# The last feed-forward group of each layer, reordered by chunk: up 0, up 1, down 0, up 2, down 1, down 2

## The chip, the core and the metric

One Trainium2 chip, one of its cores. The metric is the device time of one execution in microseconds. The engines: TensorE (PE in the profile, PEld for its weight loads), VectorE (DVE), ScalarE (ACT), GpSimd (POOL) and SyncE (SP), which issues most of the transfers.

## What is computed

One inference step of a hybrid streaming encoder with two layers, for 1024 frames of a new stream and 64 of a running one. Each layer is a mixer (attention) and a squared-ReLU MLP, each between two RMSNorms:

```
def rmsnorm(x, g):
    y = xf * lax.rsqrt(jnp.mean(xf * xf, axis=-1, keepdims=True) + NORM_EPS)
    return (y * g.astype(jnp.float32)).astype(x.dtype)

def squared_relu_mlp(h, w_up, w_down):
    u = jax.nn.relu(h @ w_up)
    return (u * u) @ w_down

xp = xp + rmsnorm(mp, g_post_mix[l])
xp = xp + rmsnorm(squared_relu_mlp(rmsnorm(xp, g_pre_ffn[l]), w_ffn_up[l], w_ffn_down[l]), g_post_ffn[l])
```

D_MODEL is 1024, D_FF 4096; after the MLP of layer 0 the norm `g_pre_mix` of layer 1 follows at once.

## The kernel before, in words

Everything is feature-major: 1088 tokens lie along the free axis, in three chunks of 384, 384 and 320 columns (`CHUNKS`). A product in float32 is made of three passes over split operands: high times high, low times high, high times low. So a weight unit of 128x1024 is loaded into a stage `WS` (three stages, `STAGE = [0, 1, 2, 0]`, so units 0 and 3 share one), cast to its high part `WH` by ScalarE (`hi_unit`, L685) and split into its low part `WL` by GpSimd (`lo_unit`, L541). There are four slots of `WH` and `WL`; a set of four units is called a quad. A load waits until the split of the unit that had its stage is over; a cast waits until TensorE has finished its last use of the slot (semaphore `D`).

The MLP runs in eight groups per layer, each over 512 of the 4096 hidden features. A group is 24 steps of 24 matmuls (L1273): 12 up steps (3 chunks of 4 units), each giving one result in PSUM, then 12 down steps, each giving two results; six PSUM banks are used in turn. VectorE empties an up result into `TU`, squares it, and makes the low part of `U` (L1200, L1203, L1206); it adds a down result to `ACC` (L1220). Before the change each quad serves all three chunks: the splits for the down quad are made during the up steps of chunk 2, those of the next group during the down steps of chunk 2.

The last group of a layer carries the norm behind the MLP as well. ScalarE squares each finished row of `ACC` into `SQ` (L715), GpSimd sums the squares (`sum_square`, L576 and L579, eight per chunk). Then for each chunk, in this order and on these engines: `post_load` (GpSimd issues the load of the residual XRES), `post_stat` (TensorE, statistics matmul, L1253), `post_st` (VectorE, L934), `post_pow` (GpSimd, power, L556), `post_dg` (VectorE, diagonal, L944), `post_bc` (TensorE, broadcast matmul, L1260), two halves of `post_x0`, `post_x1` (VectorE scales 4 rows and adds them to the residual, L953 and L958), `post_store`. In layer 0 the norm ahead of the next layer follows for each chunk: `pre_hi`, `pre_sq` (ScalarE), `pre_lo` and the reductions `pre_red0`, `pre_red1` down to `PSX` (VectorE, L963, L922, L926, L930), `pre_stat`, `pre_st`, `pre_pow`, `pre_dg`, `pre_bc`, `pre_rb`. Then the projections of layer 1 (section T0) begin.

Where each piece stands on its engine is fixed by a table: `PLAN` gives a tick for each piece, `LATER` an offset by chunk, and each engine calls `norm_at` or (TensorE) `norm_until` between its own steps, one step per tick; tick 0 of chunk 0 is the first down step of chunk 1. Each engine works strictly in its written order, and semaphores release it.

## Time and profile before

| | us |
|---|---|
| median of 3 runs | 3023.59 |
| lowest and highest | 3022.15, 3024.40 |
| the profiled execution | 3024.18 |
| its span | 3022.4 |

The page gives, over the span, TensorE busy 2836.2 us (94%), VectorE 1446.0 (48%), ScalarE 854.1 (28%), GpSimd 686.5 (23%), and 210.32 MB moved at a mean of 70 GB/s. Line L1273 (all dense matmuls) makes up 69% of the chain that ended last. Times in the rows below are counted from the span's start: layer 0's last feed-forward group begins at 1434.53, layer 1's at 2892.03.

### The profile page before, as it was taken

To read this page: it belongs to the slowest core of one execution; us is meant where nothing else is said; L and a number is where in the kernel's file an instruction comes from. 1 tells how busy PE (TensorE), PEld (TensorE's weight loads), DVE (VectorE), ACT (ScalarE), POOL (GpSimd) and SP (SyncE) were. 2 spreads that over 40 slices of the span, in tenths; PEclk is the share of its full clock that TensorE was granted. 3 is DMA by queue.
4 is the path that set the end of the run, shared out by engine and by line. 5 is a ranking of instruction groups with operands and counts; after the bars stand their busy time and mean duration, and the time that the engine had idled before them with its cause. 6 is when DMAs were issued, how large, how long until landed. Compare 5 with 4: busy or idle time off the path is not lost.

```text
span 3022.4 us, 49537 instructions
## 1 busy us (share of the span) xinstructions
PE 2836.2 (94%) x18736; PEld 2711.3 (90%) x18736; DVE 1446.0 (48%) x3541; ACT 854.1 (28%) x1561; POOL 686.5 (23%) x436
## 2 busy tenths in 40 slices
PE   5799999998999999999979999998889999999996
PEld 5788888888999999999978888887889999999996
DVE  4466655555633333333385566555573333333334
ACT  3344433354211111111233333335431111111121
POOL 1111210155211212122231110005432212122123
PEclk8899999999999999999989999999999999999998
DMA  4211211233201111010231121113411111010103
GB/s 149 99 56 55 73 70 74 87 111 141 82 35 49 35 49 56 28 56 35 72 119 60 66 96 57 57 57 121 157 67 56 36 49 55 28 56 35 49 36 119
DMA packets 58381, 210.32 MB, mean 70 GB/s; under 512 B 6888, under 2 KB 16496, under 8 KB 54816
## 3 DMA queue, kind: packets, MB, share of 16 engines
q1 hardware_dynamic: 54400, 168.95, 15.8%
q0 software_dynamic: 3888, 40.11, 3.3%
q8 instruction: 61, 1.00, 0.1%
q14 instruction: 32, 0.26, 0.0%
HBM read 163.36 MB, written 51.97 MB: 71 GB/s over the span
## 4 chain that ended last, share of the span: by engine, by line
PE 82%; DVE 6%; issue 4%; ACT 2%; POOL 1%; DMA 0%; DVEq 0%; ACTq 0%; POOLq 0%
PE ps L1273 69%; PE ps L1369 3%; PE ps L1387 3%; PE ps L1334 2%; DVE XL L963 1%; PE ps L1383 1%; PE ps L1344 1%; PE ps L1346 1%; DVE ACC L953 1%; PE ps L1354 1%; ACT Kh L853 1%; DVE PR L1073 1%; PE ps L1260 1%; ACT Qh L849 1%; POOL XL L630 0%
## 5 line engine op out<-in xcount | busy, mean ns | idle before, releaser
L1273 PE MATMUL ps<-XH,WH 128*128 128x384 f32 (+1 forms) x3096 | 1032.2, 333 | 51.6 <-DVE XL L963 22.3
L1273 PE MATMUL ps<-XL,WH 128*128 128x384 f32 (+1 forms) x3096 | 1035.1, 334 | 0.0
L1273 PE MATMUL ps<-XH,WL 128*128 128x384 f32 (+1 forms) x3096 | 1028.6, 332 | 0.0
L541 POOL TENSOR_TENSOR WL<-WS,WH 128x1024 fp32r<-128x1024 f32 x209 | 508.2, 2436 | 1805.3 <-ACT WH L685 1710.4
L1273 PE MATMUL ps<-U,WH 128*128 128x384 f32 (+1 forms) x3072 | 757.5, 330 | 0.0
L1273 PEld LDWEIGHTS ps<-XH,WH 128*128 128x128 f32 x3096 | 589.5, 190 | 60.4 <-issue 46.3
L1273 PEld LDWEIGHTS ps<-XL,WH 128*128 128x128 f32 x3096 | 589.6, 190 | 11.8 <-issue 11.8
L1273 PEld LDWEIGHTS ps<-XH,WL 128*128 128x128 f32 x3096 | 589.5, 190 | 9.4 <-issue 9.4
L1273 PEld LDWEIGHTS ps<-U,WH 128*128 128x128 f32 x3072 | 547.1, 189 | 0.0
L1273 PE MATMUL ps<-U,WL 128*128 128x384 f32 (+1 forms) x1536 | 506.7, 330 | 0.0
L685 ACT CAST WH<-WS 128x1024 fp32r<-128x1024 f32 x209 | 217.9, 1045 | 651.9 <-PE ps L1273 628.2
L1220 DVE TENSOR_TENSOR ACC<-ps,ACC 128x384 f32<-128x384 f32 (+1 forms) x336 | 178.2, 535 | 429.9 <-PE ps L1273 429.9
L772 ACT ACTIVATE PR<-PR,NM 128x640 f32<-128x640 f32 (+8 forms) x288 | 206.6, 717 | 376.3 <-DVE NM L1078 367.4
L1200 DVE SCALAR_TENSOR_TENSOR TU<-ps,RB 128x384 f32<-128x384 f32 (+1 forms) x192 | 102.7, 535 | 406.8 <-PE ps L1273 406.8
L1273 PEld LDWEIGHTS ps<-U,WL 128*128 128x128 f32 x1536 | 290.0, 189 | 0.0
L893 ACT ACTIVATE U<-TU 128x384 fp32r<-128x384 f32 (+1 forms) x192 | 97.6, 508 | 617.3 <-DVE TU L1200 617.3
L1073 DVE CUSTOM_DVE_ANT_0 PR<-ps,BIAS 128x640 f32<-128x640 f32 (+8 forms) x288 | 196.1, 681 | 80.5 <-issue 76.3
L1083 DVE COPY PT<-ps 128x640 f32<-128x640 f32 (+7 forms) x120 | 73.7, 623 | 200.1 <-PE ps L1369 199.8
L1369 PE MATMUL ps<-ident,PR 128*128 128x128 f32 (+1 forms) x996 | 134.2, 275 | 1.3 <-DVE M L1073 1.3
L778 ACT COPY PT<-ps 128x640 f32<-128x640 f32 (+8 forms) x160 | 85.1, 542 | 153.0 <-PE ps L1369 152.8
L1369 PEld LDWEIGHTS ps<-ident,PR 128*128 128x128 f32 (+1 forms) x996 | 116.2, 141 | 7.8 <-DVE M L1073 2.6
L1387 PE MATMUL ps<-PT,V 128*64 128x128 f32 (+1 forms) x1680 | 117.3, 280 | 2.3 <-ACT PT L778 2.3
(119 smaller groups left out, 2141.5 us busy)
## 6 DMA issues: line engine op xcount, KB each, us to landing
WS<-w_in SPq DMA_DIRECT2D x209, 512.0 KB, 4.5
k_out<-KT SPq DMA_DIRECT2D x16, 672.0 KB, 3.3
x_scr<-XRES POOLq DMA_DIRECT2D x6, 1536.0 KB, 5.5
XRES<-x_scr POOLq DMA_DIRECT2D x6, 1536.0 KB, 7.1
v_out<-VT SPq DMA_DIRECT2D x16, 544.0 KB, 4.8
o_scr<-OT SPq DMA_DIRECT2D x14, 544.0 KB, 2.7
XRES<-x_in POOLq DMA_DIRECT2D x4, 1536.0 KB, 9.4
BIAS<-nc_scr SPq DMA_DIRECT2D x8, 672.0 KB, 4.8
```

The costliest lines, as they stand in the source:

```text
L541: pool.tensor_tensor(WL[u][:, :], WS[STAGE[u]][:, :], WH[u][:, :].bitcast(f32), ALU.subtract)\
L685: act.copy(WH[u][:, :], WS[st][:, :]).then_inc(sem["whi"], 1)
L772: act.activation(PR[:, s % 2, m, 0:n], PR[:, s % 2, m, 0:n], ACT.Exp, bias=NM[:, q:q + 1], accum_out=L[:, q:q + 1]).then_inc(sem["ex"], 1)
L778: ins = act.copy(dst, src)
L893: act.activation(ct(U, c, u), TU[:, t % 2, 0:w], ACT.Square).then_inc(sem["uhi"], 1)
L1073: dve.tensor_tensor_reduce(out=PR[:, s % 2, m, 0:n].rearrange("p (b w) -> p b w", b=nb), in0=ps[:, 2 + 2 * m:2 + 2 * m + nb, 0:n // nb], i ...
L1083: ins = dve.tensor_copy(dst, src)
L1200: dve.scalar_tensor_tensor(out=TU[:, t % 2, 0:w], in0=ps[:, t % 6, 0:w], scalar=0.0, in1=RB[:, o:o + w], op0=ALU.max, op1=ALU.mult).then_i ...
L1220: dve.tensor_tensor(acc, ps[:, v % 6, 0:w], acc, ALU.add).then_inc(sem["evD"], 1)
L1273: return pe.matmul(bank[:, 0:w], wt, xt, start=m == 0, stop=m == 3 * tiles - 1, skip_group_check=False)
L1369: ins = pe.transpose(both(m)[0:v, n * P:(n + 1) * P], PR[:, k % 2, m, o:o + v], ident[:, :])
L1387: ins = pe.matmul(ps[f, 6, 0:P], V[0:v, t, f], PT[0:v, m, o // P, :], **ends)
```

## The change

The order of the 24 steps in the last group of each layer becomes up 0, up 1, down 0, up 2, down 1, down 2 by chunk. Since there are only four slots, the up quad is loaded and split again for up 2, and the down quad again for down 1 and 2. The norm pieces of chunk 0 behind the MLP and ahead of layer 1 stand four ticks earlier (`LATER`), so that they begin in up 2, and chunk 0's pre-norm stands ahead of chunk 1's post-norm in the order of jobs. The other groups keep their order. The weight list on the host gets the last eight units of each layer twice.

```diff
+def ff_steps(last):
+
+    order = (("up", 0), ("up", 1), ("dn", 0), ("up", 2), ("dn", 1), ("dn", 2)) if last else [(w, c) for w in ("up", "dn") for c in range(3)]
+    out, j = [], 0
+    for what, c in order:
+        for u in range(4):
+            out.append((what, c, u, j))
+            j += 1 if what == "up" else 2
+    return out
+
+
+def ff_quads(last):
+
+    return [1, 2, 3, 5] if last else [2, 5]
+
+
+def ff_result(last, what, c, u=0):
+    return next(j for w, k, v, j in ff_steps(last) if (w, k, v) == (what, c, u))
...
-            per = add(dict(D=36, evD=36, uhi=12, um=12, uu=12, whi=4 + nxt, wlo=4 + nxt), quad, stage_loads(range(nxt)))
-            out.append(Section("FF", layer, reps, per, units=8, f=f, last=last, nxt=nxt))
+            more = len(ff_quads(last)) - 1
+            per = add(dict(D=36, evD=36, uhi=12, um=12, uu=12, whi=4 * more + nxt, wlo=4 * more + nxt), *([quad] * more), stage_loads(range(nxt)))
+            out.append(Section("FF", layer, reps, per, units=4 + 4 * more, f=f, last=last, nxt=nxt))
...
-        for c, part in (((0, "post"), (0, "pre"), (1, "post"), (2, "post"), (1, "pre"), (2, "pre")) if n % 2 else
-                        ((0, "post"), (1, "post"), (0, "pre"), (2, "post"), (1, "pre"), (2, "pre"))) if part in NORMS[n]]
+        for c, part in ((0, "post"), (0, "pre"), (1, "post"), (2, "post"), (1, "pre"), (2, "pre")) if part in NORMS[n]]
...
-LATER = [(0, 4, 8), (-10.5, 0, 4)]
+LATER = [(-4, 4, 8), (-10.5, 0, 4)]
...
-                        load_quad(sec, i, 0)
-                        load_quad(sec, i, 4, sec.nxt)
+                        for q in range(len(ff_quads(sec.last))):
+                            load_quad(sec, i, 4 * q, 4 if q < len(ff_quads(sec.last)) - 1 else sec.nxt)
...
-                    pool.wait_ge(sem["D"], section("FF", n // 2 - 1, True).at(None, "D", 12 + 8 * (c + 1)))
+                    pool.wait_ge(sem["D"], section("FF", n // 2 - 1, True).at(None, "D", ff_result(True, "dn", c) + 8))
...
-                        for t in range(12):
-                            if t >= 8:
-                                lo_unit(sec, i, t - 8, t - 8)
-                            if sec.f == 0:
-                                norm_at(1 + 2 * sec.layer, NORM_ON_FF + t)
-                        for t in range(12):
-                            if sec.last:
-                                sum_square(2 + 2 * sec.layer, 2 * t)
-                                sum_square(2 + 2 * sec.layer, 2 * t + 1)
-                                norm_at(2 + 2 * sec.layer, t - 3)
-                            if t >= 8 and t - 8 < sec.nxt:
-                                lo_unit(sec, i, 4 + t - 8, t - 8)
+                        for p, (what, c, u, j) in enumerate(ff_steps(sec.last)):
+                            if what == "dn" and sec.last:
+                                for v in (8 * c + 2 * u, 8 * c + 2 * u + 1):
+                                    sum_square(2 + 2 * sec.layer, v)
+                            if p // 4 in ff_quads(sec.last):
+                                q = ff_quads(sec.last).index(p // 4)
+                                if 4 * q + u < sec.per["wlo"]:
+                                    lo_unit(sec, i, 4 * q + u, u)
+                            if sec.f == 0 and what == "up":
+                                norm_at(1 + 2 * sec.layer, NORM_ON_FF + p)
+                            if sec.last and p >= 11:
+                                norm_at(2 + 2 * sec.layer, p - 15)
...
+                            for k in range(2) if what == "dn" and sec.last else ():
+                                act.wait_ge(sem["evD"], sec.at(i, "evD", j + k + 1))
+                                square(2 + 2 * sec.layer, 2 * t + k, ct(ACC, c, 2 * u + k)).then_inc(sem["sqo"], 1)
+                            if p // 4 in ff_quads(sec.last):
+                                q = ff_quads(sec.last).index(p // 4)
+                                if 4 * q + u < sec.per["wlo"]:
+                                    uses = (2 if STAGE[u] == 0 else 1) * q + (2 if u == 3 else 1)
+                                    hi_unit(sec, i, 4 * q + u, u, uses, sec.at(i, "D", j + (1 if what == "up" else 2)))
+                            if sec.f == 0 and what == "up":
+                                norm_at(1 + 2 * sec.layer, NORM_ON_FF + p)
+                            if sec.last and p >= 11:
+                                norm_at(2 + 2 * sec.layer, p - 15)
...
+                        firsts = [0] + [4 * (q + 1) for q in ff_quads(sec.last)[:-1]]
+                        for p, (what, c, u, j) in enumerate(ff_steps(sec.last)):
+                            if p // 4 * 4 in firsts:
+                                weights(sec, i, 4 * firsts.index(p // 4 * 4) + u)
+                            if what == "up":
+                                if j < 6 and sec.f == 0:
+                                    pe.wait_ge(sem["evA"], sec.at(i, "evA", j - 5))
+                                else:
+                                    pe.wait_ge(sem["evD"], sec.at(i, "evD", j - 5))
+                                if sec.f == 0 and u == 0:
+                                    h_ready(1 + 2 * sec.layer, c)
+                                if sec.f == 0:
+                                    step(ps[:, j % 6, :], c, u, 1 + 2 * sec.layer, NORM_ON_FF + p)
+                                elif sec.last and p >= 11:
+                                    step(ps[:, j % 6, :], c, u, 2 + 2 * sec.layer, p - 15)
+                                else:
+                                    step(ps[:, j % 6, :], c, u)
+                                continue
                             if u == 0:
                                 pe.wait_ge(sem["uu"], sec.at(i, "uu", 4 * (c + 1)))
-                            for v in (2 * t, 2 * t + 1):
-                                pe.wait_ge(sem["evD"], sec.at(i, "evD", 7 + v))
+                            for k in range(2):
+                                pe.wait_ge(sem["evD"], sec.at(i, "evD", j + k - 5))
                                 for m in range(N_MM // 2):
                                     if sec.last and m % 6 == 0:
-                                        norm_until(2 + 2 * sec.layer, t - 4 + (v % 2) / 2 + m / N_MM)
-                                    ins = product(ps[:, v % 6, :], CHUNKS[c][1], c, u, 4 * (v % 2), m, U, 4, (U, 4))
+                                        norm_until(2 + 2 * sec.layer, p - 16 + k / 2 + m / N_MM)
+                                    ins = product(ps[:, (j + k) % 6, :], CHUNKS[c][1], c, u, 4 * k, m, U, 4, (U, 4))
...
+            if f == FF_GROUPS - 1:
+                out += out[-8:]
```

VectorE's loop is rewritten in the same manner over `ff_steps`.

GpSimd, from down 0's first sum of squares in layer 0's last group (RB is where the sums are kept, RS the power's result). Before:

```order
L576 COPY RB<-SQ 128x384
L579 TENSOR_TENSOR RB<-RB,SQ 128x384 x7
L551 DMA XRES<-x_scr 128x3072
L576 COPY RB<-SQ 128x384
L579 TENSOR_TENSOR RB<-RB,SQ 128x384
L556 TENSOR_TENSOR RS<-ST,halfpow 128x3
```

The same engine from the same place now (its lines are numbered 20 higher):

```order
L596 COPY RB<-SQ 128x384
L599 TENSOR_TENSOR RB<-RB,SQ 128x384
L561 TENSOR_TENSOR WL_55<-WS_59,WH_51 128x1024
L599 TENSOR_TENSOR RB<-RB,SQ 128x384 x2
L561 TENSOR_TENSOR WL_56<-WS_60,WH_52 128x1024
L599 TENSOR_TENSOR RB<-RB,SQ 128x384 x2
L561 TENSOR_TENSOR WL_57<-WS_61,WH_53 128x1024
L599 TENSOR_TENSOR RB<-RB,SQ 128x384 x2
L561 TENSOR_TENSOR WL_58<-WS_59,WH_54 128x1024
L571 DMA XRES<-x_scr 128x3072
L561 TENSOR_TENSOR WL_55<-WS_59,WH_51 128x1024
L576 TENSOR_TENSOR RS<-ST,halfpow 128x3
```

A split stands behind each pair of sums, and a fifth split, the first for down 1, stands between the load of the residual and chunk 0's power; before, two sums of chunk 1 stood there.

VectorE, from down 0's eight results in layer 0's last group. Before:

```order
L1220 TENSOR_TENSOR ACC<-ps,ACC 128x384 x8
L934 TENSOR_SCALAR ST<-ps 128x3
L1220 TENSOR_TENSOR ACC<-ps,ACC 128x384 x2
L944 TENSOR_SCALAR DG<-ident,RS 128x128 x3
L953 SCALAR_TENSOR_TENSOR ACC<-ACC,G,ps 128x384 x4
L958 TENSOR_TENSOR XRES<-XRES,ACC 128x1536
L1220 TENSOR_TENSOR ACC<-ps,ACC 128x384 x2
```

The same engine and place now:

```order
L1234 TENSOR_TENSOR ACC<-ps,ACC 128x384 x8
L951 TENSOR_SCALAR ST<-ps 128x3
L1216 SCALAR_TENSOR_TENSOR TU<-ps,RB 128x320
L1219 TENSOR_TENSOR TS<-TU 128x320
L1222 TENSOR_TENSOR U<-TS,U 128x320
L961 TENSOR_SCALAR DG<-ident,RS 128x128 x3
L970 SCALAR_TENSOR_TENSOR ACC<-ACC,G,ps 128x384 x4
L975 TENSOR_TENSOR XRES<-XRES,ACC 128x1536
```

Between the norm pieces stand the three passes over a result of up 2, where the two adds of a down step of chunk 1 stood.

GpSimd at chunk 1's power, from the first sum of chunk 2's squares, layer 0. Before:

```order
L576 COPY RB<-SQ 128x320
L579 TENSOR_TENSOR RB<-RB,SQ 128x320
L556 TENSOR_TENSOR RS<-ST,halfpow 128x3
L541 TENSOR_TENSOR WL_55<-WS_59,WH_51 128x1024
L579 TENSOR_TENSOR RB<-RB,SQ 128x320 x2
```

The same engine and place now:

```order
L596 COPY RB<-SQ 128x320
L599 TENSOR_TENSOR RB<-RB,SQ 128x320
L561 TENSOR_TENSOR WL_55<-WS_59,WH_51 128x1024
L576 TENSOR_TENSOR RS<-ST,halfpow 128x3
L599 TENSOR_TENSOR RB<-RB,SQ 128x320 x2
```

The first split of the next layer's weights has moved ahead of the power; in layer 1 there is no such split.

## Rows read from the trace of the kernel before

**Rows 1.** The page, part 1: busy time, share of the span, instructions.
```profile
PE 2836.2 (94%) x18736; PEld 2711.3 (90%) x18736; DVE 1446.0 (48%) x3541; ACT 854.1 (28%) x1561; POOL 686.5 (23%) x436
```

**Rows 2.** Busy time per window, end of layer 0's last group: PE, PEld, DVE, ACT, POOL.
```profile
1509.00:1524.00 15.00, 13.40 (x82) 13.14 (x80) 14.19 (x20) 7.41 (x13) 4.98 (x5) 1.00 0.08 32
...
1524.00:1540.00 16.00, 9.69 (x50) 9.46 (x51) 11.42 (x18) 4.16 (x6) 6.98 (x7) 0.68 0.53 200
...
1540.00:1553.00 13.00, 10.09 (x67) 9.77 (x66) 12.93 (x17) 9.06 (x15) 9.82 (x8) 1.00 0.22 83
```

**Rows 3.** What TensorE waited for, 1430 to 1620: total, times, longest.
```profile
PE ps L1253 <- issue: 6.3, 1, 6.3
...
PE ps L1253 <- POOL RB L579: 6.3, 1, 6.3
...
PE ps L1260 <- DVE DG L944: 5.8, 3, 2.9
```

**Rows 4.** Timeline of TensorE, both layers: start, us, what, idle before.
```profile
1434.53 0.34 PE L1273 MATMUL ps<-XH,WH 128*128 128x384 f32 x1
...
1528.75 1.41 PE L1253 MATMUL ps<-ones,RB 128*128 128x1 f32 x6 [6.34 <-issue]
...
1536.51 0.94 PE L1260 MATMUL ps<-DG,ones 128*128 128x128 f32 x6 [1.56 <-DVE DG L944]
...
1560.38 1.29 PE L1253 MATMUL ps<-ones,RB 128*128 128x1 f32 x6 [6.28 <-POOL RB L579]
...
2892.03 0.34 PE L1273 MATMUL ps<-XH,WH 128*128 128x384 f32 x1
...
2988.09 1.09 PE L1260 MATMUL ps<-DG,ones 128*128 128x128 f32 x6
...
3003.24 1.31 PE L1253 MATMUL ps<-ones,RB 128*128 128x1 f32 x6 [6.14 <-POOL RB L579]
```

**Rows 5.** Timeline of GpSimd, layer 0.
```profile
1473.57 2.40 POOL L541 TENSOR_TENSOR WL<-WS,WH 128x1024 fp32r<-128x1024 f32 x1 [35.32 <-ACT WH L685]
...
1477.09 2.40 POOL L541 TENSOR_TENSOR WL<-WS,WH 128x1024 fp32r<-128x1024 f32 x1 [1.12 <-ACT WH L685]
...
1487.55 1.00 POOL L579 TENSOR_TENSOR RB<-RB,SQ 128x384 f32<-128x384 f32 x1 [0.58 <-ACT SQ L715]
...
1489.67 1.01 POOL L579 TENSOR_TENSOR RB<-RB,SQ 128x384 f32<-128x384 f32 x1 [1.11 <-ACT SQ L715]
...
1532.76 0.88 POOL L556 TENSOR_TENSOR RS<-ST,halfpow 128x3 f32<-128x3 f32 x1
```

**Rows 6.** Timeline of VectorE, layer 0.
```profile
1471.56 0.49 DVE L1200 SCALAR_TENSOR_TENSOR TU<-ps,RB 128x320 f32<-128x320 f32 x1 [1.74 <-PE ps L1273]
...
1507.68 0.68 DVE L944 TENSOR_SCALAR DG<-ident,RS 128x128 f32<-128x128 f32 x3 [2.70 <-POOL RS L556]
...
1514.22 2.18 DVE L953 SCALAR_TENSOR_TENSOR ACC<-ACC,G,ps 128x384 f32<-128x384 f32 x4
...
1533.67 2.79 DVE L944 TENSOR_SCALAR DG<-ident,RS 128x128 f32<-128x128 f32 x3 [2.51 <-POOL RS L556]
...
1540.12 1.76 DVE L958 TENSOR_TENSOR XRES<-XRES,ACC 128x1536 f32<-128x1536 f32 x1
...
1547.35 2.61 DVE L944 TENSOR_SCALAR DG<-ident,RS 128x128 f32<-128x128 f32 x3
...
1549.88 7.40 DVE L963 SCALAR_TENSOR_TENSOR XL<-XRES,G,XH 128x384 fp32r<-128x384 f32 x8
```

**Rows 7.** Timeline of ScalarE, layer 0: a cast.
```profile
1472.46 1.04 ACT L685 CAST WH<-WS 128x1024 fp32r<-128x1024 f32 x1
```

**Rows 8.** Weight loads in 1200 to 1500, issue to landing.
```profile
DMA to landing us min/median/max: 3.3/4.2/5.7
```

**Rows 9.** Windows of 2 us; the number after POOL's is TensorE's granted clock.
```profile
1528.00:1530.00 2.00, 1.25 (x6) 1.28 (x7) 1.70 (x1) 0.27 (x1) 1.16 (x2) 0.50 0.27 49
...
1534.00:1536.00 2.00, 0.95 (x5) 0.69 (x3) 2.00 (x2) 0.00 (x0) 1.98 (x1) 0.86 0.02 6
```

More of the change, by code:

```diff
@@ L1210, in _ @@
[L1210 to L1222 removed]
+                        for p, (what, c, u, j) in enumerate(ff_steps(sec.last)):
+                            t, (o, w) = 4 * c + u, CHUNKS[c]
+                            if what == "up":
+                                dve.wait_ge(sem["D"], sec.at(i, "D", j + 1))
+                                if sec.f == 0:
+                                    scaled(1 + 2 * sec.layer, c)
+                                if t >= 2 or sec.base.get("uhi", 0):
+                                    dve.wait_ge(sem["uhi"], sec.at(i, "uhi", t - 1))
+                                dve.scalar_tensor_tensor(out=TU[:, t % 2, 0:w], in0=ps[:, j % 6, 0:w], scalar=0.0, in1=RB[:, o:o + w],
+                                                         op0=ALU.max, op1=ALU.mult).then_inc(sem["evD"], 1)
+                                dve.wait_ge(sem["evD"], sec.at(i, "evD", j + 1))
+                                dve.tensor_tensor(TS[:, t % 2, 0:w], TU[:, t % 2, 0:w], TU[:, t % 2, 0:w], ALU.mult).then_inc(sem["um"], 1)
+                                dve.wait_ge(sem["um"], sec.at(i, "um", t + 1))
+                                dve.wait_ge(sem["uhi"], sec.at(i, "uhi", t + 1))
+                                dve.tensor_tensor(ct(U, c, 4 + u), TS[:, t % 2, 0:w], ct(U, c, u).bitcast(f32), ALU.subtract)\
+                                    .then_inc(sem["uu"], 1)
+                                if sec.f == 0:
+                                    norm_at(1 + 2 * sec.layer, NORM_ON_FF + p)
+                            for k in range(2) if what == "dn" else ():
+                                dve.wait_ge(sem["D"], sec.at(i, "D", j + k + 1))
+                                acc, bank = ct(ACC, c, 2 * u + k), ps[:, (j + k) % 6, 0:w]
+                                if sec.f == 0:
+                                    dve.tensor_copy(acc, bank).then_inc(sem["evD"], 1)
+                                else:
+                                    dve.wait_ge(sem["evD"], sec.at(i, "evD", ff_result(False, "dn", c, u) + k + 1 - 36))
+                                    dve.tensor_tensor(acc, bank, acc, ALU.add).then_inc(sem["evD"], 1)
+                            if sec.last and p >= 11:
+                                norm_at(2 + 2 * sec.layer, p - 15)
@@ L1283, in weights @@
             def weights(sec, i, u):
-                per = {"ATT": 3, "FF": 8}.get(sec.kind, 0)
+                per = {"ATT": 3, "FF": sec.units}.get(sec.kind, 0)
                 pe.wait_ge(sem["wlo"], sec.pick(i, sec.unit + u + 1, per))
@@ L1456, in _ @@
                     with runs(pe, sec) as i:
-                        for t in range(12):
-                            c, u = t // 4, t % 4
-                            if t < 6 and sec.f == 0:
-                                pe.wait_ge(sem["evA"], sec.at(i, "evA", t - 5))
-                            else:
-                                pe.wait_ge(sem["evD"], sec.at(i, "evD", t - 5))
-                            if c == 0:
-                                weights(sec, i, u)
-                            if sec.f == 0 and u == 0:
-                                h_ready(1 + 2 * sec.layer, c)
-                            if sec.f == 0:
-                                step(ps[:, t % 6, :], c, u, 1 + 2 * sec.layer, NORM_ON_FF + t)
-                            else:
-                                step(ps[:, t % 6, :], c, u)
@@ L1471, in _ @@
-                        for t in range(12):
-                            c, u = t // 4, t % 4
-                            if c == 0:
-                                weights(sec, i, 4 + u)
+                        firsts = [0] + [4 * (q + 1) for q in ff_quads(sec.last)[:-1]]
+                        for p, (what, c, u, j) in enumerate(ff_steps(sec.last)):
+                            if p // 4 * 4 in firsts:
+                                weights(sec, i, 4 * firsts.index(p // 4 * 4) + u)
+                            if what == "up":
+                                if j < 6 and sec.f == 0:
[4 more added lines that the diff above has]
+                                    h_ready(1 + 2 * sec.layer, c)
+                                if sec.f == 0:
+                                    step(ps[:, j % 6, :], c, u, 1 + 2 * sec.layer, NORM_ON_FF + p)
[4 more added lines that the diff above has]
+                                continue
```

55 lines of the change are left out of this document (4 added, 51 removed).

## The prediction

> **What bounds the kernel now.** I read the page first: TensorE is busy 2836.2 us, 94% of the span [rows 1]. A change that moves no matmul out of the program can only move TensorE's idle time, so I looked for where it idles around the last feed-forward group of each layer. The windows over the end of layer 0's group show it [rows 2]: from 1509 on TensorE is busy 13.40 of 15, 9.69 of 16 and 10.09 of 13 us, while VectorE is busy 14.19, 11.42 and 12.93. The waits of TensorE there [rows 3] are all of the norm: 6.3 and 6.3 us at the statistics matmul (L1253), 5.8 us in three pieces at the broadcast (L1260). The reader should see that VectorE is nearly full there and that TensorE waits, in order, for small norm pieces at fixed places of its program.
>
> TensorE's own rows give two clocks of the stretch [rows 4]. Call the group's first matmul 0 (1434.53 in layer 0, 2892.03 in layer 1). The last statistics matmul (chunk 2) comes at 1560.38 = 125.8 in layer 0 and 3003.24 = 111.2 in layer 1. What lies behind these two has the same order before and after, so the change is worth what these two numbers move by.
>
> Step lengths: a step (24 matmuls) of chunk 2 takes 3.52 us (the splits on GpSimd follow each other at 1473.57 and 1477.09) and a result of a 384 wide down step 2.12 us, so a down step 4.24 (sums at 1487.55 and 1489.67) [rows 5]. The ninth up result is emptied at 1471.56 [rows 6], 37.03 after 0: less one step of 3.52 and 0.1 for the release, the eight before took 4.16 each. Without any wait the group takes 4.16 x 8 + 3.52 x 4 + 4.24 x 8 + 3.52 x 4 = 95.4 us, in either order.
>
> **The change, part by part.** No matmul is added. Added per layer are eight weight units: eight loads, eight casts (1.04 us on ScalarE) and eight splits on GpSimd (2.40 us) [rows 5, 7]. In the old order one set of splits has a whole group of steps to hide in; now down 0 and up 2 each have to cover one, and down 0 also has the eight sums of squares.
>
> A split is finished how late? Result emptied at 1471.56, so done by TensorE at 1471.45; split over at 1475.97: 4.5 us after the last use [rows 5, 6]. So the four splits for down 0, made during up 1 (16.6 to 33.3), end at 25.3, 29.5, 33.6 and 37.8. The next load into the shared stage 0 is issued at 37.8. Landing takes 3.3 to 5.7 us, median 4.2 [rows 8]; I take 4.7, since three go out together: 42.5. Cast 43.6, first split over at 46.1. From here GpSimd works without a pause, by its new order: three times two sums (2.12 us, taken from their spacing; 1.0 busy each) and one split, 46.1 + 3 x (2.15 + 2.4) = 59.7. The splits are over at 46.1, 50.7, 55.2 and 59.7; up 2's steps begin at 50.2, 53.8, 57.3 and 60.8, so the weights themselves come in time by 4 down to 1 us.
>
> The norm does not. **(a) Statistics of chunk 0** now stand at the start of up 2's second step, 53.8, and need the eighth sum, 57.3: TensorE idles 3.6 us. After an idle of 6.3 [rows 3] the rows show TensorE at half clock from 1528.75 to about 1534.6 (granted 0.50, then 0.86 in the window 1534 to 1536), 5.8 us in which half is lost [rows 9]; I count 2.7 us for each idle over about 2 us.
>
> **(b) Broadcast of chunk 0.** It stands three quarters into the same step: 18 matmuls of 0.147 at half clock, after a statistics matmul of 1.41, from 57.4: reached at 64.0. It needs the diagonal of VectorE, and that needs the power on GpSimd, and GpSimd's row ahead of the power is now the first split for down 1. That split needs a load that can be issued only when the fourth split above frees stage 0, at 59.7. So: issue 59.8, landed 65 (5.2, in the upper half of [rows 8], the residual's 1536 KB go out at the same time), cast 66.1, split 68.5, power 0.88 [rows 5], diagonal 0.68 [rows 6]: 70.1. Idle 6.1 us. Step 2 then ends, partly at half clock, at 73.8, step 3 at 78.6, up 2 at 82.1 where 64.3 was the count without waits.
>
> **(c) VectorE behind (b), layer 0 only.** It stands in line at the same diagonal. Then by its new order: half of the scaling 2.2, the residual add 1.8, up result 2 (three passes of 0.49 and two releases between them, some 1.9), again 4.0, up result 3, the low part of chunk 0's input (some 6 with the wait for ScalarE; it took 7.40 [rows 6]), up result 4, the first reduction (an add of the same size as the residual's, and 1.5 of waiting for ScalarE), two down results, the other two reductions: 72.0 + 4.0 + 1.9 + 4.0 + 1.9 + 6.0 + 1.9 + 3.3 + 0.9 + 1.8 = 97.7. The pre-statistics of chunk 0 stand a quarter into down 1's third step, 82.1 + 2 x 4.24 + 1.1 = 91.7. Idle 6.0, and half clock behind it: 1.4 for the statistics, 5.7 for the step's other 18 matmuls, 4.24 for the fourth step; down 1 ends at 109.0.
>
> **(d) Chunk 1.** Its statistics stand after the first step of down 2, at 113.5 with chunk 0's pre-broadcast in it, and nothing is late for them. The broadcast follows 2.6 later. Before, from the end of the statistics to the broadcast took 1530.16 to 1536.51, 6.35, of which the diagonal took 2.79 where it otherwise takes 0.68 [rows 4, 6]; without that 4.2. In layer 0 GpSimd now also has a split before the power (2.4): 6.6, so idle 4.0, and it ends at 122.6 (1.84 at half clock is my allowance). From the end of the broadcast to the last statistics took 1560.38 - 1537.45 = 22.9 before, with a diagonal of 2.61 at 1547.35 [rows 6] that is now gone: 20.4. Last statistics at about 143.0 against 125.8: **layer 0 +17.2 us**.
>
> **(e) Layer 1** has (a) and (b) but no (c): down 2's first step ends at 82.1 + 4 x 4.24 + 3.52 = 102.6; statistics 0.7, the chain 4.2, broadcast 0.9: 108.4. From there to the last statistics it took 14.1 before (2988.09 + 1.09 to 3003.24) [rows 4], with the same work on every engine. That is 122.5 against 111.2: **layer 1 +11.3 us**.
>
> **Moved for nothing.** The loads (16 of 512 KB) add 8 MB over the run on queues that stand idle there, and the order of the other groups stays. The tail behind the last statistics is the same row by row.
>
> Sum: 17.2 + 11.3 = 28.5 on the profiled execution's 3024.18, so 3052.7; the median run is 0.6 lower, so **3052 us**.
>
> A rule that could make it worse: the Trainium skill, "SBUF — State Buffer", section "Who interferes with whom", says that a VectorE instruction with two SBUF inputs, or in a two-port mode, and a GpSimd instruction that reads SBUF shut each other out, whoever starts first holding the port pair for its whole length. The trace agrees where they meet: the diagonal at 1533.67 took 2.79 us beside a split and 0.68 at 1507.68 without one [rows 6]. By that rule alone four meetings of a norm piece with a new split would cost up to 2.4 each, and the sum would be 3062 instead of 3053.
>
> **The rivals.**
> 1. *Forecast*: as summed. Bounds: loads at 3.3 instead of 4.7 and 5.2 us shorten (a) by 1.4 and (b) by 1.9, and if (a)'s idle leaves the clock up another 2.7 goes, in each layer, so -12; (c) may be 3 shorter. Upwards: splits met by VectorE at 2.1 us each (2.79 - 0.68), three times in layer 0 and once in layer 1, +8.4; first load of (b) held up 3 us more by the residual's transfer, +6. That is 3037 to 3067. Chance 0.68.
> 2. *Layer 0 gets its own back*: in the old order VectorE was the limit from 1509 to 1553 [rows 2]; with chunk 0's 18 us of norm gone earlier, the 6.3 at the last statistics disappears and (d) has no wait: 17.2 - 6.3 - 2.7 - 4.0 = +4, with layer 1 +11: 3039 at (e) in full, 3031 with (a) and (b) short. Against it: VectorE has everything of chunk 0 behind (b), so it is not early. Chance 0.12, 3028 to 3037.
> 3. *Faster*: the power isn't held by the split. It decides whether (b) is over by 60.6, when TensorE would reach it at full clock; then layer 0 loses the 6.3 at the statistics of chunk 1, the longest of its three broadcast waits, 2.9 [rows 3], and one half clock, 11.9, and layer 1 about 5: 3007. Against it: the split stands ahead of the power in GpSimd's order and its load cannot start before 59.7. Chance 0.04.
> 4. *The waits feed each other*: half clock delays the result that frees the weights, which delays the split, which delays the power; three such rounds of 5 to 8 us in layer 0 and two in layer 1 on top: 3070 to 3095. Chance 0.12.
> 5. *Nothing measurable*: the extra waits and the relief cancel, 3024. Chance 0.04.
>
> A measurement of this kernel can tell about 0.2%, 6 us. Below 3018 lie rival 3 and a share of 5: 0.05; within, 0.03; slower 0.92. The range that holds 8 in 10 reaches from rival 2's upper part over the forecast to the lower part of rival 4: 3034 to 3072.
>
> **What would show it.** (a) Statistics matmul about 57 us after each group's first matmul, 3 to 4 us idle. (b) Broadcast at about 70, idle about 6, with the split and its load ahead of the power on GpSimd. (c) In layer 0 a wait of about 6 at the first matmul that reads PSX. (d) 4 us at chunk 1's broadcast, 6 again at the last statistics. Last statistics at 143 and 122.5. Four or five stretches at granted clock 0.50 in layer 0 where there were two. The prediction is wrong if the first split for down 1 comes before 62, if up 2 has to wait for weights at every step, or if VectorE has caught up by down 2.

## The result and the profile after

| | us |
|---|---|
| before, median of 4 runs beside it | 3023.99 (3022.15 to 3025.09) |
| changed, median of 4 runs | 3049.85 (3048.40 to 3051.39) |
| ratio, 95% interval | 1.0086 (1.0069 to 1.0104) |
| profiled execution, span | 3048.4, 3046.6 |

Slower by 0.86%, 26 us; the forecast was 3052. The span grew by 24.2 us. The page after, part 1, as in [rows 1]:

```profile
PE 2840.6 (93%) x18736; PEld 2715.6 (89%) x18736; DVE 1451.7 (48%) x3541; ACT 869.5 (29%) x1577; POOL 724.7 (24%) x452
```

The matmuls are the same 18736. ScalarE and GpSimd have the 16 casts and splits more, 15 and 38 us of work; TensorE's busy time grew by 4.4 us only, so the rest of the 24.2 is idle. The same windows as in [rows 2]:

```profile
1509.00:1524.00 15.00, 13.43 (x81) 13.11 (x79) 13.36 (x19) 9.39 (x15) 6.33 (x4) 1.00 0.25 106
1524.00:1540.00 16.00, 10.35 (x49) 10.35 (x50) 8.46 (x14) 3.90 (x8) 9.22 (x9) 0.79 0.30 107
1540.00:1553.00 13.00, 9.18 (x62) 8.92 (x61) 2.20 (x7) 2.82 (x5) 6.29 (x7) 0.94 0.45 163
```

VectorE's load has gone down (12.93 to 2.20 us in the last), and TensorE is no busier for it. What TensorE waited for from 1430 to 1620, as in [rows 3]:

```profile
PE ps L1267 <- POOL RB L599: 11.9, 2, 9.4
PE ps L1274 <- DVE DG L961: 11.0, 2, 7.2
PE ps L1267 <- DVE PSX L947: 7.2, 1, 7.2
```

Statistics and broadcast again, and a new one, chunk 0's pre-statistics (which read PSX): 30.1 us against 18.4. Where they stand, in TensorE's timeline, as in [rows 4] (L1287 are the dense matmuls, L1267 statistics, L1274 broadcast):

```profile
1434.39 0.34 PE L1287 MATMUL ps<-XH,WH 128*128 128x384 f32 x1
...
1490.83 0.80 PE L1267 MATMUL ps<-ones,RB 128*128 128x1 f32 x6 [2.49 <-POOL RB L599]
...
1501.57 1.65 PE L1274 MATMUL ps<-DG,ones 128*128 128x128 f32 x6 [7.20 <-DVE DG L961]
...
1529.65 1.44 PE L1267 MATMUL ps<-ones,PSX 128*128 128x1 f32 x6 [7.22 <-DVE PSX L947]
...
1544.15 0.72 PE L1267 MATMUL ps<-ones,RB 128*128 128x1 f32 x6
...
1551.45 1.65 PE L1274 MATMUL ps<-DG,ones 128*128 128x128 f32 x6 [3.82 <-DVE DG L961]
...
1575.46 1.28 PE L1267 MATMUL ps<-ones,RB 128*128 128x1 f32 x6 [9.43 <-POOL RB L599]
...
2908.98 0.34 PE L1287 MATMUL ps<-XH,WH 128*128 128x384 f32 x1
...
2965.51 0.80 PE L1267 MATMUL ps<-ones,RB 128*128 128x1 f32 x6 [2.58 <-POOL RB L599]
...
2976.13 1.65 PE L1274 MATMUL ps<-DG,ones 128*128 128x128 f32 x6 [7.09 <-DVE DG L961]
...
3027.78 1.31 PE L1267 MATMUL ps<-ones,RB 128*128 128x1 f32 x6 [6.14 <-POOL RB L599]
```

From the group's first matmul to the last statistics: layer 0 141.07 (125.85 before, +15.2), layer 1 118.80 (111.21, +7.6). From layer 0's last statistics to the first matmul of layer 1's last group 1333.52 against 1331.65, +1.9, and from layer 1's last statistics to the end 18.8 against 19.2. With a start 0.1 earlier that is the 24.2 of the span.

GpSimd after, layer 0 (L561 split, L571 residual's load, L576 power); the splits made during down 0, which are the up set for up 2, alternate with pairs of sums. Shown are the first and the fourth of them, the residual's load, the first split for down 1 (the fifth) and the power:

```profile
1477.08 2.41 POOL L561 TENSOR_TENSOR WL<-WS,WH 128x1024 fp32r<-128x1024 f32 x1 [2.73 <-ACT WH L705]
...
1490.53 2.37 POOL L561 TENSOR_TENSOR WL<-WS,WH 128x1024 fp32r<-128x1024 f32 x1
1492.84 0.61 POOL L571 DMA_DIRECT2D XRES<-x_scr  x1
1497.62 2.33 POOL L561 TENSOR_TENSOR WL<-WS,WH 128x1024 fp32r<-128x1024 f32 x1 [4.17 <-ACT WH L705]
1499.92 0.88 POOL L576 TENSOR_TENSOR RS<-ST,halfpow 128x3 f32<-128x3 f32 x1
```

ScalarE after, the first cast for up 2 and the first for down 1:

```profile
1475.95 1.05 ACT L705 CAST WH<-WS 128x1024 fp32r<-128x1024 f32 x1 [2.69 <-DMA WS<-w_in]
...
1496.48 1.04 ACT L705 CAST WH<-WS 128x1024 fp32r<-128x1024 f32 x1 [3.74 <-DMA WS<-w_in]
```

Read backwards: the power starts when the fifth split ends, the split waits 4.17 us for its cast, the cast for its load, and the load was issued when the fourth split gave stage 0 free at 1492.9.

### The profile page after: what moved, and what is told of

It reads as the page before. It is cut to its first block, busy times and chain, and to the rows that moved or that the text cites. A ratio compares the mean times of both kernels' runs of the same rounds, so it can differ in the third digit from the quotient of the medians.

```text
span 3046.6 us, 49615 instructions
## 1 busy us (share of the span) xinstructions
PE 2840.6 (93%) x18736; PEld 2715.6 (89%) x18736; DVE 1451.7 (48%) x3541; ACT 869.5 (29%) x1577; POOL 724.7 (24%) x452
## 4 chain that ended last, share of the span: by engine, by line
PE 81%; DVE 6%; issue 5%; POOL 2%; ACT 2%; DMA 1%; DVEq 0%; ACTq 0%; POOLq 0%
PE ps L1287 67%; PE ps L1383 3%; PE ps L1401 3%; PE ps L1348 2%; DVE XL L980 2%; PE ps L1397 1%; PE ps L1358 1%; PE ps L1360 1%; DVE ACC L970 1%; POOL WL L561 1%; POOL RB L599 1%; PE ps L1274 1%; PE ps L1368 1%; ACT Kh L873 1%; DVE PR L1090 1%
## 5 line engine op out<-in xcount | busy, mean ns | idle before, releaser
L1287 PE MATMUL ps<-XH,WH 128*128 128x384 f32 (+1 forms) x3096 | 1034.5, 334 | 51.4 <-DVE XL L980 22.1
L1287 PE MATMUL ps<-XL,WH 128*128 128x384 f32 (+1 forms) x3096 | 1036.9, 335 | 0.0
L1287 PE MATMUL ps<-XH,WL 128*128 128x384 f32 (+1 forms) x3096 | 1030.3, 333 | 0.0
L561 POOL TENSOR_TENSOR WL<-WS,WH 128x1024 fp32r<-128x1024 f32 x225 | 545.9, 2430 | 1820.8 <-ACT WH L705 1726.0
L1287 PE MATMUL ps<-U,WH 128*128 128x384 f32 (+1 forms) x3072 | 755.7, 330 | 0.0
L1287 PEld LDWEIGHTS ps<-XH,WH 128*128 128x128 f32 x3096 | 591.4, 191 | 60.2 <-issue 46.1
L1287 PEld LDWEIGHTS ps<-XL,WH 128*128 128x128 f32 x3096 | 591.3, 191 | 11.8 <-issue 11.8
L1287 PEld LDWEIGHTS ps<-XH,WL 128*128 128x128 f32 x3096 | 590.9, 191 | 9.5 <-issue 9.5
L1287 PEld LDWEIGHTS ps<-U,WH 128*128 128x128 f32 x3072 | 545.9, 188 | 0.0
L1287 PE MATMUL ps<-U,WL 128*128 128x384 f32 (+1 forms) x1536 | 505.8, 329 | 0.0
L705 ACT CAST WH<-WS 128x1024 fp32r<-128x1024 f32 x225 | 234.3, 1044 | 664.9 <-PE ps L1287 628.2
L1287 PEld LDWEIGHTS ps<-U,WL 128*128 128x128 f32 x1536 | 289.1, 188 | 0.0
```

Source lines behind the costliest of these rows:

```text
L561: pool.tensor_tensor(WL[u][:, :], WS[STAGE[u]][:, :], WH[u][:, :].bitcast(f32), ALU.subtract)\
L705: act.copy(WH[u][:, :], WS[st][:, :]).then_inc(sem["whi"], 1)
L1287: return pe.matmul(bank[:, 0:w], wt, xt, start=m == 0, stop=m == 3 * tiles - 1, skip_group_check=False)
```

## Experiments

Theories. **A**: the cost is the power's place behind a split whose weights are still to be loaded. **B**: the eight extra loads, casts and splits per layer cost by themselves, wherever the norm stands. **C**: chunk 0's pre-norm stands too early for VectorE. **D**, made after the first four runs: units 0 and 3 share a stage, so in each set two loads, casts and splits lie in series. Medians of the kernel before were 3022.86 beside the first four kernels, 3024.16 beside the next four (22 executions, one of them 9620.66, which a median leaves aside), 3024.42 beside the last two; L0 and L1 are the last statistics matmul counted from the first matmul of each layer's group (125.8 and 111.2 before, 141.1 and 118.8 changed).

| kernel | us | ratio (95%) | L0, L1 |
|---|---|---|---|
| e1 power first | 3038.93 | 1.0052 (1.0035 to 1.0068) | 137.4, 111.9 |
| e2 old places | 3037.69 | 1.0049 (1.0032 to 1.0066) | 133.9, 116.8 |
| e3 four splits on VectorE | 3047.21 | 1.0083 (1.0066 to 1.0100) | 138.0, 120.3 |
| e4 e1, e3, later pre-statistics | 3030.57 | 1.0028 (1.0017 to 1.0040) | 130.1, 113.1 |
| e5 own fourth stage | 3032.95 | 1.0030 (1.0019 to 1.0042) | 133.9, 109.8 |
| e6 e2 and own stage | 3026.13 | 1.0006 (0.9996 to 1.0015) | 126.9, 110.2 |
| e7 old order, reloads | 3036.56 | 1.0042 (1.0025 to 1.0059) | 133.5, 116.3 |
| e8 e1, own stage, later pre-statistics | 3025.93 | 1.0007 (0.9998 to 1.0017) | 127.2, 109.4 |
| e9 e7 and own stage | 3023.94 | 0.9999 (0.9990 to 1.0008) | 126.7, 109.9 |
| e10 early norm in layer 1 only | 3022.75 | 0.9995 (0.9986 to 1.0004) | 125.9, 109.4 |

**e1**, the power ahead of the split of its step:

```diff
+                            if sec.last and p >= 12:
+                                norm_at(2 + 2 * sec.layer, p - 15)
                             if p // 4 in ff_quads(sec.last):
...
-                            if sec.last and p >= 11:
+                            if sec.last and p == 11:
```

> Edit: in the last group GpSimd does its norm pieces from up 2 on ahead of the split of the same step, not behind it. Theory A (the norm's power waits behind a split whose weights are still to be loaded): chunk 0's broadcast comes at about 61 us after the group's first matmul instead of 67.2, chunk 1's wait in layer 0 falls from 3.8 to about 1.5; layer 0 about 6 us shorter, layer 1 about 4: 3040 us. Theory B (the eight extra loads and splits cost the time wherever the norm stands): 3050, unchanged. Theory C (VectorE gets chunk 0's norm too early for what TensorE waits on): the wait for the pre-statistics in layer 0 grows by what the broadcast gains, and only layer 1 gains: 3046.

3038.9, A's number, but not its parts: layer 0 is 3.6 us shorter where A had 6, layer 1 6.9 where A had 4 (it is nearly back), and chunk 1's wait stayed at 3.60 where A had 1.5. In layer 0 the broadcast's wait fell from 7.20 to 0.93 us and the next wait grew from 7.22 to 10.73. TensorE of e1:

```profile
1496.65 0.94 PE L1276 MATMUL ps<-DG,ones 128*128 128x128 f32 x6 [0.93 <-DVE DG L963]
...
1527.31 1.44 PE L1269 MATMUL ps<-ones,PSX 128*128 128x1 f32 x6 [10.73 <-DVE PSX L949]
```

Counted from the group's first matmul (1435.67 in e1), the broadcast comes 6.2 us earlier than in the change (61.0 for 67.2) and the pre-statistics only 3.6 (91.6 for 95.3). VectorE of e1 shows why: the residual add, ready early, now waits for its transfer, which no one had moved.

```profile
1503.20 1.76 DVE L977 TENSOR_TENSOR XRES<-XRES,ACC 128x1536 f32<-128x1536 f32 x1 [3.39 <-DMA XRES<-x_scr]
```

At chunk 1 the power is now ahead of the split, but the split runs beside the diagonal, which took 2.76 us instead of 0.68. So what was won ahead of the power (2.4) was lost behind it. GpSimd and VectorE of e1:

```profile
1546.16 2.33 POOL L561 TENSOR_TENSOR WL<-WS,WH 128x1024 fp32r<-128x1024 f32 x1
1546.21 2.76 DVE L963 TENSOR_SCALAR DG<-ident,RS 128x128 f32<-128x128 f32 x3 [2.53 <-POOL RS L576]
```

**e2**, the new step order and its reloads, but each norm piece at its place of before:

```diff
-LATER = [(-4, 4, 8), (-10.5, 0, 4)]
+LATER = [(0, 4, 8), (-10.5, 0, 4)]
...
-        for c, part in ((0, "post"), (0, "pre"), (1, "post"), (2, "post"), (1, "pre"), (2, "pre")) if part in NORMS[n]]
+        for c, part in (((0, "post"), (0, "pre"), (1, "post"), (2, "post"), (1, "pre"), (2, "pre")) if n % 2 else
+                        ((0, "post"), (1, "post"), (0, "pre"), (2, "post"), (1, "pre"), (2, "pre"))) if part in NORMS[n]]
```

> Edit: the new order of steps with its extra loads and splits stays, but the norm's table and order of jobs are those of before (chunk 0's norm begins with down 1). Theory A: the splits have no norm to hold up, except chunk 1's power behind one split in layer 0 (+2.4): 3024 to 3029 us. Theory B: the extra loads and splits cost by themselves: 3040 or more. Theory C: as A, about 3026.

3037.7: neither A's 3024 to 3029 nor B's 3040. No split stands directly ahead of chunk 0's power here, and still 15 us are left. ScalarE of e2, the first cast for down 1:

```profile
1496.90 1.05 ACT L706 CAST WH<-WS 128x1024 fp32r<-128x1024 f32 x1 [7.71 <-DMA WS<-w_in]
```

It waits 7.71 us for a load; three splits in a row and, after one more load, a fourth follow until 1510.2, the residual's load, the sums and the power come behind them, and the broadcast waits 5.27 us where it waited 1.3. This is where theory D came from.

**e3**, the four splits made during down 0 moved to VectorE.

```diff
-                                if 4 * q + u < sec.per["wlo"]:
+                                if 4 * q + u < sec.per["wlo"] and not (sec.last and q == 1):
...
+                            if sec.last and p // 4 == 2:
+                                dve.wait_ge(sem["whi"], sec.pick(i, sec.loaded + 4 + u + 1, sec.per["wlo"]))
+                                dve.tensor_tensor(WL[u][:, :], WS[STAGE[u]][:, :], WH[u][:, :].bitcast(f32), ALU.subtract)\
+                                    .then_inc(sem["wlo"], 1)
```

> Edit: the four splits made during down 0 are done by VectorE instead of GpSimd; norm as in the change. Theory A: GpSimd is full in down 0, so its eighth sum is 4 us early now: no wait at chunk 0's statistics, and stage 0 is free about 3 to 4 us sooner, so the broadcast comes at about 63 instead of 67.2; each layer 3 to 5 us shorter: 3042 us. Theory B: the work is only moved, 3050. Theory C: layer 0 keeps its time, layer 1 gains 4: 3046.

3047.2, 3 us off the change. The statistics wait did not go (3.53 for 2.49), but that says nothing for or against "GpSimd has no room in down 0 for sums and splits": the sums now wait for squares, and the squares for VectorE, whose results stand behind its own splits, and these wait for their casts. GpSimd and VectorE of e3:

```profile
1483.52 2.17 POOL L599 TENSOR_TENSOR RB<-RB,SQ 128x384 f32<-128x384 f32 x2 [2.19 <-ACT SQ L735]
...
1484.88 1.89 DVE L1237 TENSOR_TENSOR WL<-WS,WH 128x1024 fp32r<-128x1024 f32 x1 [1.53 <-ACT WH L705]
```

It is e5, below, that settles it: there GpSimd does all sums and splits, and the statistics come without a wait. In layer 1 the broadcast of e3 waited longer, 10.10 us. There the residual's 1536 KB were sent for at 2961.15, ahead of the first weights for down 1 at 2962.3, and the cast for these came only at 2970.03, 7.7 us after the load was sent for; in layer 0, where the weights went first (1490.5 against 1491.25), it took 3.5. In the change the two went out within 0.1 us of each other, and the cast came 3.5 to 3.6 us later. These are single cases, and no run changed that order alone. It is the wait that the prediction had in its upper bound, at 3 us; the change itself did not have it.

**e4**, e1 and e3 together, the jobs' order of before, and in layer 0 chunk 0's pre-statistics and what follows them four ticks later (its low part and reductions stay early):

```diff
+... + (4 if n == 2 and c == 0 and what in SOONER or n == 2 and c == 0 and what == "pre_stat" else 0), c, what)
```

> Edit: power ahead of the split, the four splits on VectorE, and in layer 0 chunk 0's pre-statistics and what follows them (power, diagonal, broadcast) four ticks later with the old order of jobs; the input's low part and reductions stay early. Theory A and C together: no wait of over 2 us in up 2 and down 1, VectorE has chunk 0's work behind it before chunk 1's: layer 0 about 8 us and layer 1 about 6 us below the kernel before: 3010 us. Theory B: 3035 to 3045.

3030.6, nearer to B's lower end than to the 3010 of A with C. The broadcast is no longer late, but TensorE then waits for banks that VectorE empties, 1.45 us at 1517.44 and 3.68 at 1523.51, while VectorE does the low part of chunk 0's input and, after a wait for ScalarE, the first reduction: an early norm lies on VectorE between the results of up 2 and down 1. VectorE of e4:

```profile
1510.46 6.52 DVE L984 SCALAR_TENSOR_TENSOR XL<-XRES,G,XH 128x384 fp32r<-128x384 f32 x8
...
1520.25 2.65 DVE L943 TENSOR_TENSOR ACC<-ACC 128x1536 f32<-128x1536 f32 x1 [1.76 <-ACT ACC L726]
```

**e5**, the change with a stage of its own for the fourth unit in the last groups:

```diff
+        WS.append(place("WS3", z + (TOK + KCOLS) * 4, [P, 8 * P])[0])
...
+def stage_of(sec, u):
+    return 3 if sec.kind == "FF" and sec.last and u == 3 else STAGE[u]
```

> Edit: the change as it is, but in the last groups the fourth unit of each set is loaded into a stage buffer of its own, so that no load has to wait for a split of the set before. Work, order and norm places are those of the change. Theory D (the extra loads cost by the shared stage: two loads, casts and splits in series per set, with the norm behind them in order): statistics of chunk 0 without a wait, its broadcast at about 61 us after the group's first matmul instead of 67.2; layer 0 and layer 1 about 7 us shorter each: 3036 us. Theory B (the eight extra loads, casts and splits cost by their work): 3050. Theory C (chunk 0's pre-statistics stand too early for VectorE): layer 0 gains only half, 3040.

3033.0: D's number (3036) with 3 to spare, 17 us better than the change by one buffer. TensorE of e5:

```profile
1487.71 0.72 PE L1280 MATMUL ps<-ones,RB 128*128 128x1 f32 x6
...
1494.54 0.94 PE L1287 MATMUL ps<-DG,ones 128*128 128x128 f32 x6 [3.36 <-DVE DG L974]
...
1521.94 1.44 PE L1280 MATMUL ps<-ones,PSX 128*128 128x1 f32 x6 [9.02 <-DVE PSX L960]
...
1567.80 1.28 PE L1280 MATMUL ps<-ones,RB 128*128 128x1 f32 x6 [9.22 <-POOL RB L612]
```

The statistics come at 1487.71 - 1433.93 = 53.8, the place that the prediction counted without waits, and the broadcast waits 3.36 instead of 7.20. What is left in layer 0 are VectorE's 9.0 and the 9.2 behind it; layer 1 is 1.4 us faster than before the change.

**e6**, both at once: e5's stage and e2's two edits.

> Edit: new order of steps, norm in its places of before (as the run with the old places, which took 3037.7), with the stage buffer of its own for each fourth unit. Theory D: the 15 us that the old places still cost go away, since they were the split of the fourth unit that the residual's load and the power stand behind: 3025 us. Theory B: 3037, unchanged.

3026.1, D's number. With e5: at equal buffers the early places cost 7 us, all in layer 0.

**e7**, the step order and the places of before, but both sets loaded and split twice through three stages:

```diff
-    order = (("up", 0), ("up", 1), ("dn", 0), ("up", 2), ("dn", 1), ("dn", 2)) if last
+    order = (("up", 0), ("up", 1), ("up", 2), ("dn", 0), ("dn", 1), ("dn", 2)) if last
...
-                out += out[-8:]
+                out = out[:-8] + 2 * out[-8:-4] + 2 * out[-4:]
```

> Edit: the kernel before in its order of steps and norm places, with the extra work alone: in the last group the up weights are loaded, cast and split a second time ahead of up 2, and the down weights a second time ahead of down 1 (the same values, three stages as before). Theory D: here the second down set is made during down 0 and its last split ends just before the power of chunk 0 is wanted, so little is held up: 3025 to 3029 us. Theory B: eight loads and splits per layer cost 15 wherever they stand: 3037.

3036.6, B's number, against D as I had put it. But the trace speaks for a wait, not for work. ScalarE of e7, the first cast of the second down set:

```profile
1492.83 1.05 ACT L706 CAST WH<-WS 128x1024 fp32r<-128x1024 f32 x1 [5.11 <-DMA WS<-w_in]
```

TensorE of e7, chunk 0's statistics:

```profile
1507.63 1.41 PE L1268 MATMUL ps<-ones,RB 128*128 128x1 f32 x6 [4.99 <-POOL RB L600]
```

The second down set's first load could go out only behind the fourth split of the first; splits alternate with sums on GpSimd, and chunk 0's statistics waited 5 us for the last sum. I had wrongly expected that the old order would give the shared stage time enough. e9 puts the two theories against each other.

**e8**, e1 with the own stage, the jobs' order of before, and the later pre-statistics of e4: an attempt at a fast version.

> Edit: the change with power ahead of the split, the stage of its own for the fourth unit, and chunk 0's pre-statistics and later pieces four ticks later in layer 0 with the old order of jobs. Theories A, C and D together: no wait in up 2, one of under 2 us behind the residual's load, last statistics at about 124 us in layer 0 and 108 in layer 1 (125.8 and 111.2 before): 3020 us, just below the kernel before. Theory B: 3031 or more.

3025.9: not the 3020 hoped for, the same as before. The two waits of e4 that an early norm brings are here too: 3.68 us for a bank that VectorE empties behind the first reduction, and 3.59 at chunk 1's broadcast, whose diagonal took 2.76 beside a split.

**e9**, e7 with the own stage.

> The run before's order and places for every step of the last groups, the up set and the down set each loaded and split twice, and a fourth stage buffer of its own for the fourth unit. Theory D (what the eight extra loads cost is that units 0 and 3 share a stage, which puts two loads, casts and splits in series in each set): the chunk-0 statistics matmul of layer 0 comes without a wait again (5.0 us with the shared stage, none before) and the time is 3023 to 3027 us, within 0.1% of before. Theory B (eight more loads, casts and splits on ScalarE and GpSimd cost by themselves): the wait of 5.0 us stays at 4 us or more and the time is 3034 to 3038 us, as with the shared stage.

3023.9, ratio 0.9999: D, within its range; B's 3034 to 3038 is out. TensorE of e9, where e7 waited 4.99 us:

```profile
1502.78 0.72 PE L1281 MATMUL ps<-ones,RB 128*128 128x1 f32 x6
```

Sixteen loads, casts and splits more cost nothing that can be measured (the interval is about 3 us to either side) when each set has four stages, and 13 us when it has three (e7 less e9; e2 less e6 gives 12, or 13 when each is taken against the kernel before beside it).

**e10**, e8's power and stage, with chunk 0's norm at its old place in layer 0 and early in layer 1 alone:

```diff
-... t + LATER[n % 2][c] - ...
+... t + LATER[n % 2][c] + (4 if n == 2 and c == 0 else 0) - ...
```

> The changed step order with the fourth stage, GpSimd's power ahead of the split of its step, and chunk 0's norm early in layer 1's last group alone (in layer 0 at its place before the change). If theory C holds (the early norm loses only where a pre-norm for the next layer follows it, for VectorE's sake), layer 0's last statistics matmul stays at 127 us after the group's start and layer 1's comes at 109.4 against 110.2: the time is 3025 us. If the early norm is no gain in layer 1 either, 3026 to 3027. A time under 3022 would show a gain that I can't name now.

3022.7, where C's number was 3025: L0 is 125.9, as before the change, L1 109.4. That is 1.8 us less than before in layer 1, but e9, in the old order and places, has 109.9 there: 1.3 of the 1.8 is not the early norm's. The traces show what it is: behind the same idle of 1.97 us at chunk 1's statistics, the kernel before ran at half clock and e9 did not (the rows stand in the last section). 0.5 to 0.8 us (against e9 and e6) are left for the early norm. The time itself is 2 us under C's number, and layer 0's 125.9 is 1 us under the 127 expected; no run tells which of e10's edits did that. The ratio's interval, 0.9986 to 1.0004, does not tell the whole from no change. No version beat the kernel before.

Taken off one after the other, the 26 us are: the shared stage 17 (change to e5), the early places 7 (e5 to e6), and the step order with all it brings 2 (e6 to e9, inside the intervals). The shares depend on the order: with the early places taken off first they are 11 (change to e2, each against the kernel before beside it), and the stage then 13 (e2 to e6).

## Why the prediction was right

**(a) Statistics of chunk 0.** Forecast 57.3 us after the group's first matmul with 3.6 idle; measured 56.4 and 2.49 (layer 1: 56.5 and 2.58). The sequence of splits was right: the last ended at 58.5, forecast 59.7, the landing having come 1 us sooner. The half clock behind it, 2.7 us, did not come: the windows of 2 us show the granted clock at 1.00 behind this idle, and at 0.50 behind the later one.

```profile
1492.00:1494.00 2.00, 2.00 (x16) 2.00 (x15) 1.70 (x3) 0.47 (x1) 1.45 (x2) 1.00 0.11 18
...
1528.00:1530.00 2.00, 0.35 (x2) 0.35 (x2) 1.90 (x4) 0.51 (x2) 1.74 (x2) 0.50 1.03 418
1530.00:1532.00 2.00, 2.00 (x9) 2.00 (x9) 0.69 (x3) 0.99 (x2) 1.61 (x3) 0.50 0.59 229
```

**(b) Broadcast of chunk 0.** Forecast 70.1 with 6.1 idle; measured 67.2 with 7.20 (layer 1: 67.15 and 7.09). The chain was the one described: fourth split, load, cast, fifth split, power, diagonal. e1 shows what the power's place is worth (7.20 to 0.93) and e5 what the shared stage under it is (to 3.36). It came 3 us early since the load took 3.6 us from the split to the cast, not 5.2, and the splits were 1.2 ahead; it idled longer since TensorE, at full clock, arrived at 60.0 instead of 64.0. So the half clock that (a) did not bring saved nothing: TensorE only reached the wait sooner. The 2.7 us per layer that the prediction's lower bound took off for it were not there to be had.

**(c) VectorE behind it, layer 0.** Forecast 6.0 idle, 27.6 us behind the broadcast; measured 7.22 and 28.1. The sum over VectorE's rows held. e1 shows that it is not only VectorE's work: once the diagonal comes earlier, the residual's transfer is the next late thing.

**(d) Chunk 1 and the last statistics.** At the broadcast 4.0 forecast, 3.82 measured. At the last statistics 6.3 forecast, 9.43 measured: 22.4 us from the broadcast's end instead of 20.4. VectorE's passes there ran beside splits, the second residual add above all (1.76 us alone). VectorE:

```profile
1555.36 1.76 DVE L975 TENSOR_TENSOR XRES<-XRES,ACC 128x1536 f32<-128x1536 f32 x1
...
1560.05 3.94 DVE L975 TENSOR_TENSOR XRES<-XRES,ACC 128x1536 f32<-128x1536 f32 x1
1563.90 0.88 DVE L1234 TENSOR_TENSOR ACC<-ps,ACC 128x320 f32<-128x320 f32 x2
1564.70 7.65 DVE L980 SCALAR_TENSOR_TENSOR XL<-XRES,G,XH 128x384 fp32r<-128x384 f32 x8
```

GpSimd at the same time:

```profile
1559.96 2.40 POOL L561 TENSOR_TENSOR WL<-WS,WH 128x1024 fp32r<-128x1024 f32 x1
```

The add took 2.18 us more, nearly the length of the split. By the Trainium skill, "SBUF — State Buffer", section "Who interferes with whom", such a pair shuts each other out for one's whole length, and this row agrees. Where I had used the rule, four meetings at full price, it gave 3062; the kernel was 12 us under that, so this is a term to be charged where the rows meet, not by the number of splits. The stretch ahead of chunk 1's statistics was the other way off: 14.5 us from chunk 0's pre-statistics where the sum had 15.8. Layer 0 in all: +17.2 forecast, +15.2 measured. Rival 2 had the last wait disappear; it grew.

**(e) Layer 1.** +11.3 forecast, +7.6 measured. Nearly all of the difference is (b)'s earlier splits and load: the broadcast is 3 us nearer. Another 0.8 lies between it and chunk 1's statistics (31.7 us for 32.5), and the rest is as summed.

**What the sum left out.** +1.9 us from layer 0's last statistics to layer 1's last group, where the prediction had the same rows and the same time. 0.8 of it comes in the first 7 us: behind the idle of 9.43 TensorE stayed at a granted 0.50 until about 1582.1, 6.6 us after it started again, and before, behind 6.28, until about 1565.3, 4.9 us; the next broadcast came 6.92 us after the last statistics instead of 6.15. The rest stays open. The forecast of 28.5 was 22.8 and 1.9 in the trace, less 0.5 at the two ends of the span.

**How much of the close number is luck.** The sum for the two layers was 5.7 us too high, and the 1.9 that it left out made up a part. The profiled execution took 3048.40, 4.3 under the 3052.7 forecast for it; it was the fastest of its four, and only the median, 3049.85, comes within about 2 us. The waits, their places and their order were right, not each size.

What I had not named as the root, though the steps use it: the shared stage. I had charged the cost to the power's place, and e2 refuted that as the whole: the wait in (a), which is gone in e5, and the late load in (b) both come from the same buffer.

## What to carry to other kernels

When a set of weights must be loaded again within one step of work, look at the number of stages before the amount of work: here sixteen more casts and splits cost nothing measurable with four stages and 13 us with three, because the first load of a set stood behind the last split of the set before. A norm piece that is placed earlier gains only if every feeder is moved with it (weights, residual, VectorE's turn); otherwise the wait moves on to the next feeder, as in e1, where the broadcast's fell from 7.20 to 0.93 and the pre-statistics' grew from 7.22 to 10.73. And a last wait that is fed by the last chunk alone (6.1 us at layer 1's last statistics in every version) is not shortened by finishing the first chunk earlier.

## What the runs showed of the hardware

I had charged a stretch at half clock (1.2 instead of 2.4 GHz) to each idle of over 2 us. Idles of 2.49 us (the change), 3.00 (e8) and 3.36 (e5) were followed by windows at a granted 1.00; after 3.53 us (e3) and 3.82 (the change) the rows show 0.50. The windows of e3 behind its 3.53:

```profile
1490.00:1492.00 2.00, 0.45 (x5) 0.48 (x5) 0.45 (x1) 0.00 (x0) 1.86 (x2) 1.00 0.26 37
1492.00:1494.00 2.00, 2.00 (x13) 2.00 (x13) 1.49 (x4) 0.47 (x1) 0.00 (x0) 0.79 0.92 348
1494.00:1496.00 2.00, 2.00 (x9) 2.00 (x9) 0.06 (x1) 1.04 (x1) 0.86 (x1) 0.50 1.11 459
```

The length of the idle does not tell by itself, though. In layer 1, at chunk 1's statistics, TensorE idled 1.97 us in the kernel before and in e9; the first then ran at half clock for some 6 us, the second at full clock. The kernel before, then e9:

```profile
2981.87 1.41 PE L1253 MATMUL ps<-ones,RB 128*128 128x1 f32 x6 [1.97 <-issue]
2982.00:2984.00 2.00, 2.00 (x9) 2.00 (x10) 0.68 (x3) 0.07 (x1) 0.28 (x1) 0.50 0.95 393
...
2981.60 0.80 PE L1281 MATMUL ps<-ones,RB 128*128 128x1 f32 x6 [1.97 <-issue]
2982.00:2984.00 2.00, 2.00 (x16) 2.00 (x16) 0.97 (x3) 0.87 (x2) 0.43 (x2) 1.00 0.87 320
```

At the same place the same idle of 1.97 was followed by 0.50 in e7 and by 1.00 in e6, in one trace each. What decides between them no run here shows, and the effect, 1.3 us in layer 1 between the kernel before and e9, is larger than the gain that e10 was looking for there (0.8).

The second surprise was how little 8 MB more of loads disturbed: e9 moves them at no cost that can be measured. The one place where a transfer seems to have held up another is layer 1 of e3, and there it was the residual's, sent for 1.2 us ahead of the weights.
